# One 512-column matmul for x's high and low parts in the FFNs' gate and up slots

## The reference

```python
def swiglu(x, w_gate, w_up, w_down):
    return (jax.nn.silu(x @ w_gate) * (x @ w_up)) @ w_down

h = h + 0.5 * swiglu(rmsnorm_2(h, ffn1_norm[l]), ffn1_w_gate[l], ffn1_w_up[l], ffn1_w_down[l])
...
h = h + 0.5 * swiglu(rmsnorm_2(h, ffn2_norm[l]), ffn2_w_gate[l], ffn2_w_up[l], ffn2_w_down[l])
```

## Time and profile before

| | us |
|---|---|
| median of 3 runs | 1264.29 (1264.03 to 1265.34) |
| the profiled execution | 1262.68 |
| its span, first to last instruction | 1260.9 |
| TensorE busy in it | 1205.3 (96%) |
| VectorE, ScalarE, GpSimd busy | 702.9, 647.4, 694.2 |
| mean granted TensorE clock | 0.968 |

### The profile page before, as it was taken

How to read it: one execution, slowest core, us unless ns; L and a number is a source line. 1 busy time by engine, 2 the same in 40 slices (tenths; PEclk the granted TensorE clock), 3 DMA queues, 4 the chain that set the end, 5 groups by cost and what they waited for, 6 DMA issues and landing times.

```text
span 1260.9 us, 25550 instructions
## 1 busy us (share of the span) xinstructions
PE 1205.3 (96%) x9388; PEld 1137.8 (90%) x9388; DVE 702.9 (56%) x1181; ACT 647.4 (51%) x1009; POOL 694.2 (55%) x549
## 2 busy tenths in 40 slices
PE   7999999999989999899998999998999898999997
PEld 6987997999978789799998999998979897999997
DVE  4559786667544787847764333234256575434443
ACT  5653664465547357635645444444556434444442
POOL 4535565456754345735565666665565554666661
PEclk9989999999989899999997999998999997999998
DMA  5633345455634333545365556654444544565550
GB/s 201 209 126 112 116 127 183 147 159 177 205 116 139 121 118 117 168 140 169 133 206 187 178 191 198 194 193 146 134 145 142 166 149 136 168 194 190 198 198 35
DMA packets 57288, 199.56 MB, mean 158 GB/s; under 512 B 6352, under 2 KB 9456, under 8 KB 57072
## 3 DMA queue, kind: packets, MB, share of 16 engines
q1 hardware_dynamic: 53520, 193.95, 46.8%
q10 hardware_dynamic: 3680, 4.42, 1.1%
HBM read 196.52 MB, written 1.84 MB: 157 GB/s over the span
## 4 chain that ended last, share of the span: by engine, by line
PE 66%; POOL 10%; DVE 9%; issue 9%; ACT 3%; DMA 2%; SPq 0%; POOLq 0%; DVEq 0%; ACTq 0%
PE ps L1317 38%; PE ps L1337 12%; POOL ring L255 10%; PE ps L1327 6%; PE ps L1301 2%; DMA raw<-in_w 2%; PE ps L1468 2%; DVE ring L757 1%; ACT ring L361 1%; PE ps L1435 1%; DVE ca L1032 1%; PE ps L1305 1%; DVE gs L945 1%; DVE y L778 0%; DVE rms L747 0%
## 5 line engine op out<-in xcount | busy, mean ns | idle before, releaser
L255 POOL TENSOR_TENSOR ring<-raw,ring 128x512 fp32r<-128x512 f32 x484 | 648.0, 1361 | 476.5 <-ACT ring L361 475.5
L1317 PE MATMUL ps<-xs,ring 128*128 128x256 f32 x5760 | 699.9, 282 | 14.6 <-ACT xs L375 7.7
L1317 PEld LDWEIGHTS ps<-xs,ring 128*128 128x128 f32 x5760 | 679.6, 191 | 32.0 <-issue 16.5
L361 ACT ACTIVATE ring<-raw 128x1024 fp32r<-128x1024 f32 x364 | 383.7, 1055 | 201.6 <-DMA raw<-in_w 90.0
L757 DVE TENSOR_TENSOR ring<-raw,ring 128x1024 fp32r<-128x1024 f32 x122 | 165.1, 1353 | 244.2 <-ACT ring L361 242.9
L1337 PE MATMUL ps<-ys,ring 128*128 128x256 f32 x2016 | 237.7, 277 | 2.7 <-DVE ys L788 2.7
L1337 PEld LDWEIGHTS ps<-ys,ring 128*128 128x128 f32 x2016 | 233.2, 188 | 3.2 <-issue 3.2
L1327 PE MATMUL ps<-ring,xs 128*128 128x512 f32 x480 | 123.9, 412 | 4.6 <-DVE ca L1032 4.6
L1327 PEld LDWEIGHTS ps<-ring,xs 128*128 128x128 f32 x480 | 91.3, 195 | 26.9 <-issue 7.3
L622 ACT ACTIVATE ex<-ps 128x256 f32<-128x256 f32 x44 | 16.9, 384 | 68.0 <-PE ps L1317 68.0
L1032 DVE SCALAR_TENSOR_TENSOR ca<-ps,par,ca 128x253 f32<-128x253 f32 (+2 forms) x96 | 45.0, 477 | 12.2 <-ACT ca L421 10.7
(11 more groups left out here) (240 smaller groups left out, 986.2 us busy)
## 6 DMA issues: line engine op xcount, KB each, us to landing
raw<-in_w SPq DMA_DIRECT2D x364, 512.0 KB, 3.3
y<-bias_rows ACTq DMA_DIRECT2D x6, 256.0 KB, 3.3
x<-in_x SPq DMA_DIRECT2D x1, 1024.0 KB, 7.8
out_y<-y SPq DMA_DIRECT2D x4, 256.0 KB, 2.3
const<-in_const SPq DMA_DIRECT2D x1, 896.0 KB, 11.9
bias_rows<-lg ACTq DMA_DIRECT2D x1, 768.0 KB, 5.8
par<-in_par ACTq DMA_DIRECT2D x3, 181.0 KB, 2.4
dec<-in_wT ACTq DMA_DIRECT2D x1, 512.0 KB, 3.6
```

The costliest lines, as they stand in the source:

```text
L255: last = pool.tensor_tensor(ring[:, g % RING, 1, half], raw[:, g % RAW, half], ring[:, g % RING, 0, half].bitcast(F32), ALU.subtract)
L361: act.activation(ring[:, g % RING, 0, :], raw[:, g % RAW, :], ACT.Copy).then_inc(S["hi"], 1)
L1317: last = mm(ps[bank][:, half * T:(half + 1) * T], ring[:, slot % RING, wp, (at + k) * P:(at + k + 1) * P], rhs(k, xp), start=(i == 0), sto ...
```

## The change

In gate and up slots of both FFNs, `wide_product` takes the place of `tile_product`. The weight tile's high part meets `xs[:, k, 0:2, :]`, high and low parts side by side, in one matmul of 512 columns that fills the whole bank; the weight's low part meets x's high part in one of 256 columns, added to columns 0 to 255. Each slot has 8 + 8 = 16 matmuls. Columns 256 to 511 then hold weight high by x low, and the two halves are added on the way out: ScalarE copies columns 256 to 511 to `mq` (unused in an FFN), VectorE adds columns 0 to 255 to that. For the gate the sum goes to `mq[:, 4 + f % 2, :]`, and tanh and the (tanh + 1) * z step read it there; for the up slot it goes to `ca`. With `ready`, both parts of x's tile k are waited for before the first matmul of k.

```diff
--- before.py
+++ after.py
@@ -195,6 +195,15 @@
         relu = lg[:, :, :].rearrange("p a t -> p (a t)").rearrange("p (b e n) -> p b e n", b=2, e=2)
         relu4 = lg[:, :, :].rearrange("p a t -> p (a t)").rearrange("p (h n) -> p h n", h=4)
         pT = gs
+
+        def gate_x(f):
+            return mq[:, f % 2, :]
+
+        def up_x(f):
+            return mq[:, 2 + f % 2, :]
+
+        def gate_sum(f):
+            return mq[:, 4 + f % 2, :]
         hot = emr[0:32, :, :].rearrange("p a t -> p (a t)")[:, 0:HOT]
 
         ps = [ctx.enter_context(nc.psum_tensor(f"ps{b}", [P, 512], F32)) for b in range(8)]
@@ -211,7 +220,7 @@
         gout gout_ev gsq gssq gvar grms idx_ps idx_relu idx_used pen
         dsq dssq dvar drms dqk_in dl_ps dl dl_max dl_e dl_p dT dT_ev dpv dpv_ev
         conv_out conv_e mqk_in ms mp mnum hj hsq hssq hvar hrms
-        sum_out x_new ffn_e ffn_h a_ps a_max a_e a_p a_T a_T_ev a_pv a_pv_ev
+        sum_out x_new ffn_e ffn_h ffn_g ffn_u ffn_t a_ps a_max a_e a_p a_T a_T_ev a_pv a_pv_ev
         wT_in wT_cut ln_in ge_t ge_e ge_done ln_v ln_r vln sg sg_done mo_e merged stored""".split()
         S = {n: sem(n) for n in names}
         slot_in = [sem(f"slot_in{s}") for s in range(RAW)]
@@ -619,10 +628,15 @@
                         act.wait_ge(S["slots_used"], i * per + (p + 1))
                         if f >= 2:
                             act.wait_ge(S["ffn_h"], i * fs + (h_done + f - 1))
-                        act.activation(ex[:, f % 2, :], ps[2 * (f % 2)][:, 0:T], ACT.Tanh, scale=0.5)\
-                            .then_inc(S["ffn_e"], 1)
+                        act.activation(gate_x(f), ps[2 * (f % 2)][:, T:2 * T], ACT.Copy).then_inc(S["ffn_g"], 1)
+                    elif what == "up":
+                        act.wait_ge(S["slots_used"], i * per + (p + 1))
+                        act.activation(up_x(f), ps[2 * (f % 2) + 1][:, T:2 * T], ACT.Copy).then_inc(S["ffn_u"], 1)
                     if p + RING < TOTAL_SLOTS:
                         split(p, i, per)
+                    if what == "gate":
+                        act.wait_ge(S["ffn_t"], i * fs + (h_done + f + 1))
+                        act.activation(ex[:, f % 2, :], gate_sum(f), ACT.Tanh, scale=0.5).then_inc(S["ffn_e"], 1)
                     if what == "up":
                         act.wait_ge(S["ffn_h"], i * fs + (h_done + f + 1))
                         act.activation(ys[:, f % 2, 0, :], ca[:, f % 2, :], ACT.Copy).then_inc(S["y_hi"], 1)
@@ -1144,16 +1158,21 @@
                 def part(f, what, p, i=0, per=0, fs=0):
 
                     e = f % 2
+                    if what == "gate":
+                        dve.wait_ge(S["ffn_g"], i * fs + (h_done + f + 1))
+                        tt(gate_sum(f), gate_x(f), ps[2 * e][:, 0:T], ALU.add).then_inc(S["ffn_t"], 1)
+                    elif what == "up":
+                        dve.wait_ge(S["ffn_u"], i * fs + (h_done + f + 1))
+                        step(tt(ca[:, e, :], up_x(f), ps[2 * e + 1][:, 0:T], ALU.add))
                     if p + RING < TOTAL_SLOTS:
                         split(p, i, per)
                     if what == "gate":
 
                         dve.wait_ge(S["ffn_e"], i * fs + (h_done + f + 1))
-                        step(stt(ex[:, e, :], ex[:, e, :], 1.0, ps[2 * e][:, 0:T], ALU.add, ALU.mult))
+                        step(stt(ex[:, e, :], ex[:, e, :], 1.0, gate_sum(f), ALU.add, ALU.mult))
                     elif what == "up":
 
-                        dve.wait_ge(S["slots_used"], i * per + (p + 1))
-                        tt(ca[:, e, :], ex[:, e, :], ps[2 * e + 1][:, 0:T], ALU.mult).then_inc(S["ffn_h"], 1)
+                        tt(ca[:, e, :], ex[:, e, :], ca[:, e, :], ALU.mult).then_inc(S["ffn_h"], 1)
                         split_y(ca[:, e, :], e, i * fs + (y_done + f + 1))
 
                 def two(i, per, fs, j=0):
@@ -1317,6 +1336,21 @@
                     last = mm(ps[bank][:, half * T:(half + 1) * T],
                               ring[:, slot % RING, wp, (at + k) * P:(at + k + 1) * P], rhs(k, xp),
                               start=(i == 0), stop=(i == len(order) - 1))
+                return last
+
+            def wide_product(bank, slot, ready):
+
+                for k in range(KT):
+                    if ready:
+                        ready(k, 0)
+                        ready(k, 1)
+                    for wp in (0, 1) if k == 0 else (1, 0):
+                        w = ring[:, slot % RING, wp, k * P:(k + 1) * P]
+                        if wp == 0:
+                            last = mm(ps[bank][:, :], w, xs[:, k, :, :].rearrange("p a t -> p (a t)"),
+                                      start=(k == 0), stop=(k == KT - 1), skip_group_check=True)
+                        else:
+                            mm(ps[bank][:, 0:T], w, xs[:, k, 0, :], start=False, stop=False, skip_group_check=True)
                 return last
 
             def value_slot(banks, slot, q):
@@ -1620,8 +1654,7 @@
                 def gate_up(f, slot, arrived, ready=None):
                     for half in range(2):
                         arrived(slot + half)
-                        tile_product(2 * (f % 2) + half, 0, slot + half, xs_part, ready=ready)\
-                            .then_inc(S["slots_used"], 1)
+                        wide_product(2 * (f % 2) + half, slot + half, ready).then_inc(S["slots_used"], 1)
 
                 gate_up(0, at, here, norm_ready(n))
                 gate_up(1, at + 2, here)
```

## The result

The changed kernel takes 1272.69 us (median of 11 executions, 1271.26 to 1277.27), the kernel before 1266.09 us (11 executions, 1261.18 to 1274.93). The ratio is 1.0052, with a 95% interval of 1.0027 to 1.0077: slower by 0.3 to 0.8%. The forecast was 1265.6 in a range of 1260.0 to 1268.2.

What follows compares the result with a forecast made beforehand. TensorE's matmul stream was taken to bound the FFNs; +2.0 + 0.3 - 0.2 - 0.3 - 0.5 = +1.3 us on the profiled 1262.7 gave 1264.0, or 1265.6 on the median's scale, range 1260.0 to 1268.2.

Steps and rivals of the forecast that it cites:

- The bound: Through both FFNs TensorE alone sets the time, 8.16 us a tile; the other engines only have to be in time.
- The matmul stream: Gate and up slots: 704 wide matmuls at 229.3 ns, each 2.8 ns over two narrow ones, +2.0 us in all.
- TensorE's sum slots stay at 2.72 us: Expected of the profile after, in both FFNs: sum slots keep their 2.72 us.
- My bound from above: Matmul stream: if the 34 value-slot matmuls hide nothing and the reading is off by 2 ns, +3.4 us.
- A price per matmul: Faster rival: 6.6 ns come with each matmul or weight load, stream -4.7 us, total 1260.3 us; chance 0.22.
- The rule of the Trainium skill: Warm back-to-back matmuls start every N / 2.4 GHz plus about 2.5 ns; by it -7.6 us with measured narrow ones; not adopted.
- A wide matmul dearer than the value slots': Slower rival: a wide matmul takes, say, 235 ns, +6.0 - 0.7, total 1269.6 us; chance 0.04.
- The evacuation: Added copies and additions on ScalarE and VectorE: steady state 0, first FFN's end +0.3 us, second FFN's end 0.
- `y_lo` came in time: Forecast: 0.3 to 1.3 us later, covered by 4.3 us; slower rival, late in second FFN, chance 0.04.
- as feared of operations beside GpSimd: VectorE's (tanh + 1) * z and product, reading SBUF only, may take 1.3 us in place of 0.42.
- the +0.3 forecast: End of first FFN: the new copy stands ahead of the split in the chain, so the last sum slot waits 0.3 us longer.
- The start and the clock: First gate slots end earlier, -0.2 and -0.3 us; clock return absorbs lateness in mixing block and second FFN, -0.5 us.

Runs made afterwards that it cites:

- wides-first kernel: The change with each slot's 8 matmuls of 512 columns first, then the 8 of 256; 1268.68 us, ratio 1.0012 to the kernel before.
- narrow-halves kernel: The change with its new evacuation, but each 512-column matmul made two of 256 columns; 1264.69 us, ratio 0.9972 to the kernel before.
- first look: The kernel before, unchanged, profiled once more; one execution, 1263.03 us.
- second look: The kernel before, unchanged, profiled again for the same question; one execution, 1278.88 us.
- two narrow last: The change's alternating order, but each slot ends in three wide and then two narrow matmuls; 1275.19 us, ratio 1.0074 to the kernel before.
- 15 wides: The change with one wide matmul of each up slot (k = 3) as two narrow ones; 1276.10 us, ratio 1.0092 to the kernel before.
- both alternating seeds: Change's order only in four slots ahead of each FFN's loop, narrow halves inside: 1278.27 us; same with one wide matmul less per seed: 1275.88 us.

## Why the prediction was wrong

**The bound: right.** TensorE alone sets the FFNs' time after the change too, and nothing waits mid-FFN.

**The matmul stream: the step that failed**, "704 x 2.8 = +2.0 us". A tile takes 8.445 us in place of 8.16, and 44 of them make +12.5 us. The wide matmul's price was taken from the value slots and set beside narrow ones at 113.3 ns, as if each had a price of its own. What has a price is the pace, and in the change both FFNs were at the slow one. Gate and up slots take 8.445 - 2.83 = 5.615 us a tile in place of 5.44: +7.7 us, where I had 2.0. The sum had no term at all for slots that the change doesn't touch: 44 sum slots at 2.83 in place of 2.72 us are +4.8 us, and "TensorE's sum slots stay at 2.72 us" is where the profile contradicts the prediction most plainly. My bound from above, +3.4 us, allowed for 2 ns on the wide matmul and for no change of pace. The wides-first kernel shows how much goes with order: with 16 matmuls a slot as in the change, a tile is 0.11 us over before's, 4.8 us in all, and the other 7.7 are the alternation's.

**A price per matmul, the rival that I gave 0.22: wrong.** In no order did a wide matmul come to 220 ns; the least was 225 to 226, two narrow ones at 113.3, and with eight in a row the mean was 231 to 232.5. The rule of the Trainium skill, page "TensorE: Matmul & The Clock Gate", section "Wait — 56ns, not 53.3ns?", a fixed 2.5 ns per warm matmul, isn't borne out by fp32r matmuls here: they carry 6.6 or 11.1 ns over their columns at 256, and 12 to 22 at 512. "A wide matmul dearer than the value slots'", say 235 ns, was the closest, at 0.04, by luck: 235 is what two narrow ones take at the slow pace, which this rival didn't have in mind, and the sum slots are missing from it.

**The evacuation: right.** The narrow-halves kernel has all of it and is at 0.9972 (0.9941 to 1.0003). `y_lo` came in time in all tiles; VectorE's (tanh + 1) * z did take 1.3 us in the first FFN, as feared of operations beside GpSimd, and it was hidden. At the end of the first FFN, from the sum slot 20's start to the last one's, it was 866.57 - 862.59 = 3.98 us, and after the change:

```profile
868.78 2.99 PE L1371 MATMUL ps<-ys,ring 128*128 128x256 f32 x24
872.97 2.98 PE L1371 MATMUL ps<-ys,ring 128*128 128x256 f32 x24 [1.19 <-DVE ys L802]
```

4.19 us: +0.2, but half of it is sum slot 20 at the slow pace. The wait itself grew from 1.10 to 1.19 us, +0.1 for the +0.3 forecast. In the second FFN it is hidden, as forecast: 48 matmuls in 5.82 us without a gap.

**The start and the clock: right in sign, too small.** After the change the clock is back about 3.7 us after the first matmul of the first FFN (686.84), before it was more than 5.8 us after the earlier trace rows:

```profile
689.00:690.00 1.00, 1.00 (x5) 0.50 0.09 16
690.00:691.00 1.00, 1.00 (x5) 0.73 0.80 82
691.00:692.00 1.00, 1.00 (x7) 1.00 0.62 246
```

From the sum of squares to the first sum slot, each FFN gave back 1.4 us (22.3 us after, 23.7 before), where I had 0.2 and 0.3 at the starts and 0.5 for two norms' clocks. But none of this is shown to be the change's: the kernel before took 22.0 us there in both FFNs of its first look, with the clock at 0.50 for 10.2 us, as after the change, in place of the 13.7 us in the profile that the rows are from, and 25.6 us in the second FFN of its second look.

The mixing block's 2.2 us lie at its end, and not in its norm. Before, ScalarE stands at a split whose load hasn't landed, and squares x for the sum of squares only after it:

```profile
1053.95 1.06 ACT L361 ACTIVATE ring<-raw 128x1024 fp32r<-128x1024 f32 x1 [2.80 <-DMA raw<-in_w]
...
1055.58 6.15 PE L1301 MATMUL ps<-const,y 128*128 128x1 f32 x32 [2.59 <-ACT y L366]
```

TensorE waits 2.59 us for it. After the change it waits 0.60 us, and the kernel before, in its first look, 0.64:

```profile
1059.83 4.49 PE L1320 MATMUL ps<-const,y 128*128 128x1 f32 x32 [0.60 <-ACT y L375]
```

```profile
1057.85 4.21 PE L1301 MATMUL ps<-const,y 128*128 128x1 f32 x32 [0.64 <-ACT y L366]
```

So this gain, too, comes and goes without the change.

**What stays open:** why a matmul has two paces at one granted clock. The runs show what leads to which, not by what means. An idle wait can end in either one: behind the wait at the end of the first FFN, of 1.2 to 1.4 us, the change went from 117.8 to 113.3 ns, and the kernel before, in its second look, from 113.3 to 117.8. An alternating stretch ends in 117.8 in all ten FFNs profiled (the change, two narrow last, 15 wides, both alternating seeds); eight wide ones in a row and then narrow ones end in 113.3 in all four. The rule that every wide matmul flips it is refuted by two kernels.

## What to carry to other kernels

Where TensorE sets the time, read the pace of its matmuls from start to start in every stage, with the code unchanged too, before pricing a change: the same instruction can have two prices that last for 100 us and more, and a change of a few matmuls' order can choose between them. Here, one matmul of 512 columns in place of two of 256 brought nothing, and mixing the widths one by one put the stream and what follows at the pace that is 4% slower. Where two widths are needed, try them grouped, and read the pace again. When a kernel's own executions spread by 1%, profile more than one before taking its trace for the kernel.

## What the runs showed of the hardware

- At a granted clock of 1.00, fp32r matmuls of 256 columns start every 113.3 or every 117.8 ns. Either pace holds for a whole loop of 20 tiles, 163 or 170 us, through 1,440 matmuls.
- Wide ones of 512 columns, with `xs` moving, take 226, 231 or 236 ns to the next start: the sum of two such paces. The mean is 229 in the value slots, 231 to 232.5 in runs of eight, 235 between narrow ones.
- Which pace a uniform stream has can be settled by what stands ahead of it, 64 matmuls at most: ten FFNs behind an alternating stretch at 117.8, four behind wides first at 113.3, and narrow ones alone behind a norm at either, in different executions of one program.
